# Two-layer hybrid decoder trunk on one core: stick-breaking sums in wider matmuls, a stacked short block of the latents, and another order of VectorE's and GpSimd's work between the output projection and the MLP

## The chip, the cores and the metric

One core of a Trainium2 chip runs one program. The metric is the device time of one execution in microseconds (us). The kernel before was timed in three runs: median 666.29, lowest 665.9, highest 666.32. PE is TensorE, DVE is VectorE, ACT is ScalarE, POOL is GpSimd, SP is the engine that issues most of the transfers.

## The reference, cut to what matters

Two layers (DEPTH = 2) over 256 tokens (two token tiles of 128) of width 1024. Each layer has four head groups of 4 heads x 64, one output projection, a gated MLP with a causal convolution, and a gated per-layer embedding. Three places of a layer matter here:

```python
# group A: stick-breaking attention
log_keep = jnp.where(mask, jax.nn.log_sigmoid(-z), 0.0)
shifted = jnp.concatenate([log_keep[..., 1:], jnp.zeros_like(log_keep[..., :1])], axis=-1)
tail = lax.cumsum(shifted, axis=3, reverse=True)
w = jnp.where(mask, jnp.exp(log_beta + tail), 0.0)
# group B: latents of rank 192 (queries) and 128 (keys, values), normalised, then projected up
c_q = rms_norm(mla[..., :192], mla_q_norm[i]);  c_kv = rms_norm(mla[..., 192:320], mla_kv_norm[i])
q_m = c_q @ mla_w_uq[i];                        kv_m = c_kv @ mla_w_ukv[i]
# between the attention and the MLP
x = x + groups.reshape(B, S, MIX_WIDTH) @ w_o[i]
h = rms_norm(x, ffn_norm[i])                    # then h @ w_up[i]
# at the end of a layer; p @ ple_proj can be computed at any time before
x = x + (p[i] @ ple_proj[i]) * jax.nn.sigmoid(x @ ple_gate[i])
```

## The kernel before, in words

**Weights.** All weights arrive in "units" of at most 128 x 2048 f32 through six slots of `raw`. A weight is used as two float32r numbers: ACT copies `raw` into a rounded high part (`high(u)`, L592), and DVE (`low(u)`, L1715) or POOL (`low(u)`, L460, for the units from `U_POOL` on) subtracts it from `raw` and leaves the low part in `wl`. A product of two such split operands is three matmuls into one sum (`split_product`, L966 to L968): high by high, high by low, low by high. Each engine has its own written order of instructions, with waits on counting semaphores (`F[...]`); nothing reorders them at run time.

**Stick-breaking sums (PE, L1298 to L1318).** With keys on the partitions, the sums along the keys are matmuls by a constant triangle `neg_tri_r` and, for the later key tile, a constant block `neg_ones_r`. Banks 4 and 5 of PSUM hold two heads each, 256 columns a head; bank 6 holds the four heads' later tile. For each bank and each of its two heads there are four matmuls: triangle by `sp_h` and by `pt_r` (256 columns each), ones by the high and the low part of the later tile (128 columns each). Bank 6 follows with two matmuls of 512 columns. ACT then takes the exponentials. PE goes on with `mla_T(1)` (L1286), the projection `M_SWA_B`, the first group's values (L1331), the scores, `o_turned`, transposes, the unit `M_MOBA_V`, and `group_T(0)` (L1342), which waits for `group_done`, made by DVE's `group_norm(0)` (L1811) after a root by POOL (L452). POOL comes to that root after `low(U_WO)` (L460) and two roots of other groups.

**Latents.** DVE scales the 192 and 128 columns (L1871, two instructions a token tile, `lat_done`); PE transposes them in three blocks of 128, 64 and 128 columns (L1226); ACT copies them as high parts `cT_h`, DVE subtracts for low parts `cT_l` (L1883). The second block has 64 rows of data and is multiplied with 128 rows of `uq`, of which POOL sets the lower 64 to zero. Each token tile takes 3 + 3 matmuls of 384 columns for the queries and 3 of 512 for keys and values.

**From the output projection to the MLP (the middle).** Four quarters of x (token tile, half of the columns) lie in PSUM banks 0 to 3. DVE adds each to x (`add_to_x`, L2003), ACT squares it with a sum (`x_square`, L573), and for each token tile POOL adds two sums (L467), makes the mean (L447) and takes the power -0.5 (L470; `x_root`). DVE's `norm(1)` writes hn = x * root * gain by quarters (L1652), PE transposes them (`x_T`, L1018), ACT and DVE make high and low parts, and the first unit of the MLP (`up(0, 0)`, L1504) starts. DVE's order is: addition 0, `low(U_FFN)` (a whole unit), additions 1 to 3, then the four hn. Between, PE has the product p @ ple_proj as filling: `project_p(0)`, `project_p(1)`, x_T of quarters 0 and 1, `project_p(2)`, x_T of quarters 2 and 3, `project_p(3)`; each `project_p` is six matmuls of 512 columns.

Of the kernel before, what the change touches and what calls it, by code (L numbers as in the profile page):

```python
# [15 lines left out]
P = 128  # L16
# [5 lines left out]
H = 4  # L22
# [16 lines left out]
MLA_COLS = QR + KVR + PE_DIM  # L39

# [64 lines left out]
def _cols(n):  # L105
# [25 lines left out]
    "x_squared": 8, "roots": 15, "hn_ready": 4, "xT_ready": 12, "hT_ready": 4, "roots_wide": 1, "row_root": 1,  # L131
    "xT_high": 12, "xT_low": 12, "pr_ready": 6, "squared": 7, "sums_ready": 4, "ssk_ready": 1,
    "lat_done": 2, "lat_T": 2, "cT_ready": 2, "mla_up": 2, "mla_up_ready": 4, "v_ready": 6,
    "mla_qk": 2, "mla_T": 2, "mT_ready": 4, "rrow_ready": 1, "uq_zero": 1, "up_high": 2, "up_low": 2, "cT_low": 2, "proj_high": 2, "proj_low": 2, "mla_high": 1, "mla_low": 1, "mla_a_high": 1, "mla_a_low": 1, "sbq_high": 1, "sbq_low": 1, "moba_qk": 1,
# [8 lines left out]
    "x_done": 4, "tables": 1, "sg_landed": 16, "uq_landed": 16, "uq2_landed": 16,  # L143
# [29 lines left out]
def build(nc, x_in, p_cols, positions, w_in, w_uq, w_ukv, attn_cols, norm_gains,  # L173
          small_gains, w_o, w_up, conv_cols, w_down, ple_proj, ple_gate, out):
    with ExitStack() as ctx:
# [241 lines left out]
        def _(pool):  # L417
# [36 lines left out]
            for layer in range(DEPTH):  # L454
# [50 lines left out]
                if layer == 0:  # L505
                    pool.memset(uq[QR - P:P, 1, :], 0.0).then_inc(consts_made, 1)
                    pool.wait_ge(consts_made, 13)
                    for z in (qk_sb, qk_moba, qk_swa):
                        pool.memset(z[:, 0:H, :], 0.0).then_inc(consts_made, 1)
                    pool.wait_ge(consts_made, 16)  # L510
# [57 lines left out]
        def _(act):  # L568
            act.dma_start(gcol[:], attn_cols).then_inc(gcol_landed, 16)
            def x_square(i):  # L570

                t, c = quarter(i)
                return act.activation(hn[:, t, c], x[:, t, c], ACT.Square,  # L573
                                      accum_out=stat(ST_X + i))

            for layer in range(DEPTH):
# [142 lines left out]
                act.wait_ge(F["uq2_landed"], base["uq2_landed"] + 16)  # L719
                act.wait_ge(F["ukv_landed"], base["ukv_landed"] + 16)  # L720
                if layer == 0:
                    act.wait_ge(consts_made, 13)
                else:
                    act.wait_ge(F["uq_zero"], layer)
# [221 lines left out]
        def _(pe):  # L946
            pe.sem_inc(w_used, RING)
            pe.wait_ge(consts_made, 12)
            for layer in range(DEPTH):
# [273 lines left out]
                for t in range(TT):  # L1223
                    pe.wait_ge(F["lat_done"], base["lat_done"] + t + 1)
                    for n, (c, w) in enumerate(((0, P), (P, QR - P), (QR, KVR))):
                        mm = pe.transpose(ps[0:w, 4 + t, n * P:(n + 1) * P], pr[:, 0, t, c:c + w],  # L1226
                                          ident[:])
                    mm.then_inc(F["lat_T"], 1)
                project_T(M_SB_K, 3, columns=(1,))
                if layer == 0:  # L1230
                    pe.wait_ge(consts_made, 16)
# [68 lines left out]
                for b in range(2):  # L1300
                    for j in range(2):
                        i = 2 * b + j
                        h = PAIRED[i]
                        o = ps[:, 4 + b, j * 256:(j + 1) * 256]
                        pe.matmul(o, neg_tri_r[:], sp_h[b][:, j * 256:(j + 1) * 256],
                                  start=False, stop=False, skip_group_check=True)
                        pe.matmul(o, neg_tri_r[:], pt_r[:, i * 256:(i + 1) * 256],
                                  start=False, stop=False, skip_group_check=True)
                        pe.matmul(o[:, P:256], neg_ones_r[:], sp_h[2][:, h * P:(h + 1) * P],
                                  start=False, stop=False, skip_group_check=True)  # L1310
                        mm = pe.matmul(o[:, P:256], neg_ones_r[:],
                                       pt_r[:, 1024 + h * P:1024 + (h + 1) * P], start=False,
                                       stop=True, skip_group_check=True)
                    mm.then_inc(F["sb_minus"], 1)
# [146 lines left out]
                def project_p(n):  # L1461
# [3 lines left out]
                    for k in range(2):  # L1465
# [4 lines left out]
                                           k == 0, k == 1)  # L1470
                    if n < 3:
# [107 lines left out]
        def _(dve):  # L1579
# [64 lines left out]
            for layer in range(DEPTH):  # L1644
                base = before(layer)
                def norm(n):
# [59 lines left out]
                def low(u, halves=False):  # L1706

                    slot, n, c = u % DEEP, COLS[u], 0
                    if halves:
# [6 lines left out]
                       ALU.subtract).then_inc(l_made, 1)  # L1716

# [150 lines left out]
                for t in range(TT):  # L1868
                    for j, (c, w, g) in enumerate(((0, QR, S_QN), (QR, KVR, S_KVN))):
                        v = pr[:, 0, t, c:c + w]  # L1870
                        last = stt(v, v, stat(ST_L + 4 + 2 * j + t), sg[:, g:g + w], ALU.mult,  # L1871
                                   ALU.mult)
# [7 lines left out]
                for t in range(TT):  # L1880
                    dve.wait_ge(F["cT_ready"], base["cT_ready"] + t + 1)
                    tok = slice(t * P, (t + 1) * P)
                    tt(cT_l[:, :, tok], ps[:, 4 + t, 0:384].rearrange("p (k n) -> p k n", k=3),  # L1883
                       cT_h[:, :, tok].bitcast(F32), ALU.subtract).then_inc(F["cT_low"], 1)
# [8 lines left out]
                if layer == 0:  # L1893
                    dve.wait_ge(consts_made, 16)
# [213 lines left out]
```

## Time and profile before

| what | value |
| --- | --- |
| time, median of 3 runs | 666.29 us |
| profiled execution: its own time | 666.2 us |
| profiled execution: span, first to last instruction | 664.5 us |
| time outside the span | 1.7 us |
| mean granted clock of PE | 0.998 |
| busy in the span: PE, DVE, ACT, POOL | 654.1, 436.1, 423.8, 414.0 us |

The time outside of the span is taken as it is. PE matmuls are pipelined, so what a matmul costs is read from the distance between the starts of two neighbours and not from its duration. The start of each row is in us from the start of the span; the second layer repeats the first some 326.5 us later.

### The profile page before, as it was taken

Reading aid. Unit: us, or ns where it says so; the run is one execution under the profiler, and the core shown is the slowest. Engines: PE = TensorE matmul, PEld = TensorE weight load, DVE = VectorE, ACT = ScalarE, POOL = GpSimd, SP = SyncE. Lnnn points to the kernel's source line nnn. Section 1 sums busy time; section 2 is a strip of 40 time slices with the busy share of each in tenths; the row PEclk is TensorE's granted clock in tenths of the full one; section 3 lists DMA queues with packets and bytes.
Section 4 is the critical chain, followed back from the end, with each engine's and each line's share of the span. In section 5 each row is a group of like instructions: output and inputs, shape, how many; then the busy total and the mean of one; then the engine's idle time right before and its main releaser. Section 6 shows DMA issues by size and latency. Waiting matters only on the chain.

```text
span 664.5 us, 9585 instructions
## 1 busy us (share of the span) xinstructions
PE 654.1 (98%) x3800; PEld 563.4 (85%) x3800; DVE 436.1 (66%) x621; ACT 423.8 (64%) x633; POOL 414.0 (62%) x222
## 2 busy tenths in 40 slices
PE   7999999999999999999999999999999999999997
PEld 5988887888888888888889889878888888888885
DVE  6976878749898985003488588875688989910033
ACT  6669886676767675334474889746776767643342
POOL 5543610388888887987841373015888888889871
PEclk9999999999999999999999999999999999999999
DMA  9962134575555555553387421165555555555411
GB/s 321 374 232 64 66 109 160 186 236 190 190 189 191 191 190 189 190 190 107 108 292 236 157 96 66 65 205 176 190 190 190 190 191 190 191 190 189 159 33 63
DMA packets 74445, 115.18 MB, mean 173 GB/s; under 512 B 2336, under 2 KB 58272, under 8 KB 74144
## 3 DMA queue, kind: packets, MB, share of 16 engines
q1 hardware_dynamic: 73248, 111.75, 50.6%
q10 hardware_dynamic: 1152, 2.81, 1.2%
q8 instruction: 30, 0.49, 0.3%
q14 instruction: 15, 0.12, 0.1%
HBM read 113.51 MB, written 1.05 MB: 172 GB/s over the span
## 4 chain that ended last, share of the span: by engine, by line
PE 94%; DVE 4%; ACT 1%; DMA 1%; issue 0%; POOL 0%; ACTq 0%
PE ps L1515 24%; PE ps L966 14%; PE ps L968 14%; PE ps L967 14%; PE ps L1517 12%; PE ps L1018 2%; PE ps L1112 1%; PE ps L1138 1%; PE ps L980 1%; PE ps L1377 1%; DVE wl L1715 1%; PE ps L1053 1%; PE ps L1150 1%; DVE hn L2068 1%; PE ps L1538 1%; PE ps L1540 1%
## 5 line engine op out<-in xcount | busy, mean ns | idle before, releaser
L460 POOL TENSOR_TENSOR wl<-raw,wh 128x2048 fp32r<-128x2048 f32 (+1 forms) x74 | 333.6, 4514 | 81.4 <-ACT wh L592 81.4
L1515 PE MATMUL ps<-hT_hl,wh 128*128 128x512 f32 x688 | 238.6, 392 | 0.0
L592 ACT ACTIVATE wh<-raw 128x2048 fp32r<-128x2048 f32 (+1 forms) x102 | 186.1, 1828 | 76.8 <-PE ps L968 69.7
L1517 PE MATMUL ps<-hT_hl,wl 128*128 128x256 f32 x688 | 193.6, 281 | 0.0
L1515 PEld LDWEIGHTS ps<-hT_hl,wh 128*128 128x128 f32 x688 | 129.2, 188 | 28.0
L1517 PEld LDWEIGHTS ps<-hT_hl,wl 128*128 128x128 f32 x688 | 129.6, 188 | 0.0
L447 POOL TENSOR_SCALAR st<-st 128x2 f32<-128x2 f32 (+3 forms) x26 | 11.1, 428 | 113.3 <-ACT lat L667 61.2
L966 PE MATMUL ps<-wh,hT_hl 128*128 128x512 f32 (+1 forms) x216 | 79.8, 369 | 0.0
L968 PE MATMUL ps<-wh,hT_hl 128*128 128x512 f32 (+1 forms) x216 | 77.4, 359 | 0.0
L967 PE MATMUL ps<-wl,hT_hl 128*128 128x512 f32 (+1 forms) x216 | 77.4, 358 | 0.0
L2003 DVE TENSOR_TENSOR x<-x,ps 128x512 f32<-128x512 f32 x16 | 10.6, 686 | 99.5 <-PE ps L968 97.5
L1715 DVE TENSOR_TENSOR wl<-raw,wh 128x2048 fp32r<-128x2048 f32 (+1 forms) x28 | 57.6, 2062 | 0.1
L968 PE MATMUL ps<-wh,g_late 128*128 128x512 f32 x144 | 56.1, 389 | 0.0
L967 PE MATMUL ps<-wl,g_late 128*128 128x512 f32 x144 | 56.1, 389 | 0.0
L966 PE MATMUL ps<-wh,g_late 128*128 128x512 f32 x144 | 56.0, 389 | 0.0
L2032 DVE SCALAR_TENSOR_TENSOR pb<-ps,conv,pb 128x255 f32<-128x255 f32 (+1 forms) x96 | 39.6, 473 | 17.3 <-ACT pb L888 17.3
L966 PEld LDWEIGHTS ps<-wh,hT_hl 128*128 128x128 f32 x216 | 40.8, 189 | 7.2 <-DVE wl L1715 1.1
L968 PEld LDWEIGHTS ps<-wh,hT_hl 128*128 128x128 f32 x216 | 40.8, 189 | 6.1
L967 PEld LDWEIGHTS ps<-wl,hT_hl 128*128 128x128 f32 x216 | 40.8, 189 | 5.3
L2045 DVE TENSOR_TENSOR g_late<-pb,g_late 128x512 fp32r<-128x512 f32 x10 | 38.4, 3841 | 3.8 <-ACT g_late L901 3.8
L2045 DVE TENSOR_TENSOR g_late<-pt,g_late 128x512 fp32r<-128x512 f32 x8 | 37.0, 4629 | 2.4 <-ACT g_late L901 2.4
L879 ACT ACTIVATE qk_moba<-ps 128x512 f32<-128x512 f32 x22 | 13.2, 599 | 38.3 <-PE ps L1517 38.3
(311 smaller groups left out, 1177.0 us busy)
## 6 DMA issues: line engine op xcount, KB each, us to landing
raw<-w_up SPq DMA_DIRECT2D x44, 1024.0 KB, 5.1
raw<-w_down SPq DMA_DIRECT2D x22, 1024.0 KB, 4.8
raw<-w_in SPq DMA_DIRECT2D x16, 1024.0 KB, 8.9
raw<-w_o SPq DMA_DIRECT2D x6, 1024.0 KB, 5.0
raw<-ple_gate SPq DMA_DIRECT2D x6, 1024.0 KB, 4.9
raw<-w_in SPq DMA_DIRECT2D x4, 704.0 KB, 5.3
ng<-norm_gains ACTq DMA_DIRECT2D x2, 1024.0 KB, 6.7
raw<-w_o SPq DMA_DIRECT2D x4, 512.0 KB, 4.1
```

Of the source, the lines that this page charges most:

```text
L460: pool.tensor_tensor(wl[:, slot, 0:n], raw[:, slot, 0:n], w_high(u)[:, 0:n].bitcast(F32), ALU.subtract).then_inc(done, 1)
L592: act.activation(w_high(u)[:, c:n], raw[:, slot, c:n], ACT.Copy).then_inc(h_made, 1)
L879: act.activation(low_halves[half], ps[:, bank:bank + 2, SEQ:2 * SEQ], ACT.Copy).then_inc(F["low_copied"], 1)
L966: pe.matmul(dst, a_h, b_h, start=start, stop=False, skip_group_check=True)
L967: pe.matmul(dst, a_h, b_l, start=False, stop=False, skip_group_check=True)
L968: return pe.matmul(dst, a_l, b_h, start=False, stop=stop, skip_group_check=True)
L1018: mm = pe.transpose(ps[:, banks[k], j * P:(j + 1) * P], src[:, t, c:c + P], ident[:])
L1515: pe.matmul(both, high[:, c], hU_all[:, k].rearrange("p a n -> p (a n)"), start=k == 0, stop=False, skip_group_check=True)
L1517: mm = pe.matmul(o, wl[:, slot, c], hU_h[:, k, :], start=False, stop=k == KT - 1, skip_group_check=True)
L1715: tt(wl[:, slot, c:n], raw[:, slot, c:n], w_high(u)[:, c:n].bitcast(F32), ALU.subtract).then_inc(l_made, 1)
L2032: stt(o, ps[:, bank + j, 0:SEQ - d], conv[:, tap, f:f + 1], o, ALU.mult, ALU.add).then_inc(F[name], 1)
L2045: tt(g_low(s), cv[s % 2][:, 0:2, :], g_high(s).bitcast(F32), ALU.subtract).then_inc(F["g_low"], 1)
```

## The change

1. **Stick-breaking sums.** For banks 4 and 5, the two heads of a bank go in one matmul: four a bank instead of eight; columns 512, 512, 256, 256, the latter two with two pieces of 128 columns each in the moving operand and in PSUM.
2. **Latents.** The 64 columns of the short block are written twice beside each other (`LAT_TWICE`), so that its transpose has 128 rows; DVE turns the lower 64 rows of `cT_h` into the low part in place. `uq` is loaded into both halves by two transfers. The block's product is two matmuls instead of three. POOL's zero fill of `uq`, with ACT's waits for it, goes away. DVE has three instructions a token tile where L1871 had two, and two where L1883 had one.
3. **The middle, DVE and POOL.** DVE adds quarters 0, 1, 2, makes the first half of the first MLP unit's low part (`low_part(U_FFN, 0)`), adds quarter 3, and then does `norm`: the sum of two squares and the constant for tile 0 (`x_mean(0)`), hn of quarters 0 and 1, `x_mean(1)`, the second half of the low part, hn of quarters 2 and 3. POOL has only the power there. ACT squares with a scale of D ** -0.5, so that the sum is a mean.
4. **The middle, PE.** The first three matmuls of `project_p(2)` come ahead of x_T of quarters 0 and 1.

```diff
 def load_small(eng, layer):
-            eng.dma_start(uq[0:QR - P, 1, :], w_uq[layer][P:QR, :]
-                          ).then_inc(F["uq2_landed"], 16)
+            for rows in (slice(0, QR - P), slice(QR - P, P)):
+                eng.dma_start(uq[rows, 1, :], w_uq[layer][P:QR, :]).then_inc(F["uq2_landed"], 16)
...
 # POOL
                 def x_root(n, t):
-                    pool.wait_ge(F["x_squared"], base["x_squared"] + 4 * n + 2 * t + 2)
-                    chained(pool.tensor_tensor(stat(ST_X + 4 + t), stat(ST_X + 2 * t),
-                                               stat(ST_X + 2 * t + 1), ALU.add))
-                    chained(mean(ST_X + 4 + t, 1, D))
+                    if n:
+                        pool.wait_ge(F["mean_ready"], base["mean_ready"] + t + 1)
+                    else:
+                        pool.wait_ge(F["x_squared"], base["x_squared"] + 2 * t + 2)
+                        chained(pool.tensor_tensor(stat(ST_X + 4 + t), stat(ST_X + 2 * t),
+                                                   stat(ST_X + 2 * t + 1), ALU.add))
+                        chained(mean(ST_X + 4 + t, 1, 1))
                     pool.tensor_tensor(stat(ST_X + 6 + t), stat(ST_X + 4 + t), neg_half[:, 0:1],
                                        ALU.pow).then_inc(F["roots"], 1)
...
-                if layer:
-                    pool.wait_ge(F["tables"], layer + 1)
-                    pool.memset(uq[QR - P:P, 1, :], 0.0).then_inc(F["uq_zero"], 1)
-                    pool.wait_ge(F["uq_zero"], layer)
...
 # PE, latents
-                    for n, (c, w) in enumerate(((0, P), (P, QR - P), (QR, KVR))):
-                        mm = pe.transpose(ps[0:w, 4 + t, n * P:(n + 1) * P], pr[:, 0, t, c:c + w],
+                    for n, c in enumerate((0, LAT_TWICE, QR)):
+                        mm = pe.transpose(ps[:, 4 + t, n * P:(n + 1) * P], pr[:, 0, t, c:c + P],
                                           ident[:])
...
-                    for k in range(2):
-                        split_product(o, cT_h[:, k, tok], cT_l[:, k, tok], uq_h[:, k, :],
-                                      uq_l[:, k, :], k == 0, k == 1)
+                    split_product(o, cT_h[:, 0, tok], cT_l[:, 0, tok], uq_h[:, 0, :],
+                                  uq_l[:, 0, :], True, False)
+                    pe.matmul(o, cT_h[:, 1, tok], uq_h[:, 1, :], start=False, stop=False,
+                              skip_group_check=True)
+                    pe.matmul(o, cT_h[0:QR - P, 1, tok], uq_l[0:QR - P, 1, :], start=False,
+                              stop=True, skip_group_check=True)
...
 # PE, stick-breaking sums
                 for b in range(2):
-                    for j in range(2):
-                        i = 2 * b + j
-                        h = PAIRED[i]
-                        o = ps[:, 4 + b, j * 256:(j + 1) * 256]
-                        pe.matmul(o, neg_tri_r[:], sp_h[b][:, j * 256:(j + 1) * 256],
-                                  start=False, stop=False, skip_group_check=True)
-                        pe.matmul(o, neg_tri_r[:], pt_r[:, i * 256:(i + 1) * 256],
-                                  start=False, stop=False, skip_group_check=True)
-                        pe.matmul(o[:, P:256], neg_ones_r[:], sp_h[2][:, h * P:(h + 1) * P],
-                                  start=False, stop=False, skip_group_check=True)
-                        mm = pe.matmul(o[:, P:256], neg_ones_r[:],
-                                       pt_r[:, 1024 + h * P:1024 + (h + 1) * P], start=False,
-                                       stop=True, skip_group_check=True)
-                    mm.then_inc(F["sb_minus"], 1)
+                    o = ps[:, 4 + b, :]
+                    later = o.rearrange("p (j n) -> p j n", j=2)[:, :, P:SEQ]
+                    high, low = (sp.rearrange("p (h n) -> p h n", h=H)[:, b:b + 3:2, :]
+                                 for sp in (sp_h[2], pt_r[:, 1024:1536]))
+                    pe.matmul(o, neg_tri_r[:], sp_h[b], start=False, stop=False,
+                              skip_group_check=True)
+                    pe.matmul(o, neg_tri_r[:], pt_r[:, b * 512:(b + 1) * 512], start=False,
+                              stop=False, skip_group_check=True)
+                    pe.matmul(later, neg_ones_r[:], high, start=False, stop=False,
+                              skip_group_check=True)
+                    pe.matmul(later, neg_ones_r[:], low, start=False, stop=True,
+                              skip_group_check=True).then_inc(F["sb_minus"], 1)
...
 # PE, the middle
                 project_p(1)
+                project_p(2, (0,))
                 x_T(hn, AT_MIDDLE, ("hn_ready", 0), quarters=(0, 1))
-                project_p(2)
+                project_p(2, (1,))
...
 # DVE, the middle
+                    def x_mean(t):
+                        dve.wait_ge(F["x_squared"], base["x_squared"] + 4 * n + 2 * t + 2)
+                        stt(stat(ST_X + 4 + t), stat(ST_X + 2 * t), EPS, stat(ST_X + 2 * t + 1),
+                            ALU.add, ALU.add).then_inc(F["mean_ready"], 1)
+                    x_mean(0)
                     for i in range(4):
                         t, c = quarter(i)
+                        if i == 2:
+                            x_mean(1)
+                            between()
...
-                add_to_x("wo_done", U_PROJ - 1, "x_mid", (0,))
-                low(U_FFN)
-                add_to_x("wo_done", U_PROJ - 1, "x_mid", (1, 2, 3))
-                norm(1)
+                add_to_x("wo_done", U_PROJ - 1, "x_mid", (0, 1, 2))
+                low_part(U_FFN, 0)
+                add_to_x("wo_done", U_PROJ - 1, "x_mid", (3,))
+                norm(1, lambda: low_part(U_FFN, 1))
```

## Rows read from the trace of the kernel before

**Rows 1.** The page: the chain that ended last, by engine.

```profile
PE 94%; DVE 4%; ACT 1%; DMA 1%; issue 0%; POOL 0%; ACTq 0%
```

**Rows 2.** Who waited for whom, PE: us in total, times, longest.

```profile
PE ps L1018 <- DVE hn L1652: 0.8, 2, 0.4
```

**Rows 3.** Timeline and windows, stick-breaking sums: start, duration; the window's length and busy times.

```profile
59.33 0.33 PE L1305 MATMUL ps<-gT_h,neg_tri_r 128*128 128x256 f32 x1
59.50 0.28 PE L1307 MATMUL ps<-pt_r,neg_tri_r 128*128 128x256 f32 x1
59.62 0.22 PE L1309 MATMUL ps<-gT_l,neg_ones_r 128*128 128x128 f32 x1
59.68 0.28 PE L1311 MATMUL ps<-pt_r,neg_ones_r 128*128 128x128 f32 x1
...
58.84:61.23 2.39, 2.39 (x20) 2.24 (x19) 2.36 (x2) 2.39 (x4) 1.32 (x1) 1.00 0.52 122
```

**Rows 4.** Timeline, latents of layer 0: DVE's scaling and low parts, PE's products.

```profile
24.05 1.73 DVE L1871 SCALAR_TENSOR_TENSOR pr<-pr,st,sg 128x192 f32<-128x192 f32 x4 [0.80 <-POOL st L452]
...
27.85 1.01 DVE L1883 TENSOR_TENSOR pt_r<-ps,pb_r 128x384 fp32r<-128x384 f32 x2
...
30.02 0.34 PE L966 MATMUL ps<-uq_h,pb_r 128*128 128x384 f32 x1
30.20 0.34 PE L967 MATMUL ps<-uq_l,pb_r 128*128 128x384 f32 x1
```

**Rows 5.** Timeline, the middle of layer 0, all engines.

```profile
116.72 0.69 DVE L2003 TENSOR_TENSOR x<-x,ps 128x512 f32<-128x512 f32 x1 [1.01 <-PE ps L1377]
...
117.33 2.28 DVE L1715 TENSOR_TENSOR wl<-raw,wh 128x2048 fp32r<-128x2048 f32 x1
...
118.11 0.39 PE L968 MATMUL ps<-wh,hT_hl 128*128 128x512 f32 x1
...
119.53 1.88 DVE L2003 TENSOR_TENSOR x<-x,ps 128x512 f32<-128x512 f32 x3
119.69 0.39 PE L966 MATMUL ps<-proj_h,pT_h 128*128 128x512 f32 x1
...
121.05 0.19 POOL L467 TENSOR_TENSOR st<-st 128x1 f32<-128x1 f32 x1 [9.65 <-ACT hn L573]
...
121.60 0.56 POOL L470 TENSOR_TENSOR st<-st,neg_half 128x1 f32<-128x1 f32 x1
...
122.19 1.41 DVE L1652 SCALAR_TENSOR_TENSOR hn<-x,st,ng 128x512 f32<-128x512 f32 x2 [0.79 <-POOL st L470]
122.27 0.72 POOL L467 TENSOR_TENSOR st<-st 128x1 f32<-128x1 f32 x1
...
124.07 0.47 PE L966 MATMUL ps<-proj_h,pT_h 128*128 128x512 f32 x1
...
124.33 1.41 DVE L1652 SCALAR_TENSOR_TENSOR hn<-x,st,ng 128x512 f32<-128x512 f32 x2 [0.73 <-POOL st L470]
...
126.33 0.47 PE L966 MATMUL ps<-proj_h,pT_h 128*128 128x512 f32 x1
...
127.80 0.28 PE L1504 MATMUL ps<-hT_hl,wh 128*128 128x256 f32 x1
```

**Rows 6.** Timeline: POOL's short operations beside VectorE's long ones, both layers.

```profile
59.86 2.29 DVE L1715 TENSOR_TENSOR wl<-raw,wh 128x2048 fp32r<-128x2048 f32 x1
59.91 2.31 POOL L447 TENSOR_SCALAR st<-st 128x16 f32<-128x16 f32 x1 [14.73 <-DVE st L1732]
...
337.03 0.88 POOL L470 TENSOR_TENSOR st<-st,neg_half 128x1 f32<-128x1 f32 x1
```

**Rows 7.** Timeline before group_T(0), layer 0: POOL, DVE and PE.

```profile
68.16 5.14 POOL L460 TENSOR_TENSOR wl<-raw,wh 128x2048 fp32r<-128x2048 f32 x1 [0.45 <-ACT wh L592]
...
75.87 0.88 DVE L1811 SCALAR_TENSOR_TENSOR hn<-ps,st,ng 128x256 f32<-128x256 f32 x2 [0.95 <-POOL st L452]
...
77.08 0.60 PE L1342 MATMUL ps<-ident,hn 128*128 128x128 f32 x4
```

More of the change, by code:

```diff
@@ L39 @@
 MLA_COLS = QR + KVR + PE_DIM
+LAT_TWICE = 384
 SB, MLA, SWA, MOBA = range(4)
@@ L572, in x_square @@
                 t, c = quarter(i)
-                return act.activation(hn[:, t, c], x[:, t, c], ACT.Square,
+                return act.activation(hn[:, t, c], x[:, t, c], ACT.Square, scale=D ** -0.5,
                                       accum_out=stat(ST_X + i))
@@ L718, in _ @@
                 act.wait_ge(F["uq_landed"], base["uq_landed"] + 16)
-                act.wait_ge(F["uq2_landed"], base["uq2_landed"] + 16)
+                act.wait_ge(F["uq2_landed"], base["uq2_landed"] + 32)
                 act.wait_ge(F["ukv_landed"], base["ukv_landed"] + 16)
[L721 to L724, printed above, removed]
                 for o, w in ((uq_h, uq), (ukv_h, ukv)):
@@ L1230, in _ @@
                 if layer == 0:
-                    pe.wait_ge(consts_made, 16)
+                    pe.wait_ge(consts_made, 15)
                 pe.wait_ge(F["up_low"], base["up_low"] + 2)
@@ L1459, in _, with project_p @@
                 project_out(3, (3,))
-                def project_p(n):
+                def project_p(n, blocks=range(2)):
                     slot, _ = unit(U_PROJ)
                     t, half = divmod(n, 2)
-                    for k in range(2):
+                    for k in blocks:
                         c = slice(k * D + half * 512, k * D + half * 512 + 512)
@@ L1470, in project_p @@
                                            k == 0, k == 1)
+                    if k == 0:
+                        return
                     if n < 3:
@@ L1645, in _, with norm @@
                 base = before(layer)
-                def norm(n):
+                def norm(n, between):
+                    def x_mean(t):
[3 more added lines that the diff above has]
+                    x_mean(0)
                     for i in range(4):
                         t, c = quarter(i)
+                        if i == 2:
+                            x_mean(1)
+                            between()
                         dve.wait_ge(F["roots"], base["roots"] + 13 * n + t + 1)
@@ L1716, in low, with low_part @@
                        ALU.subtract).then_inc(l_made, 1)
+                def low_part(u, part):
+                    slot, n = u % DEEP, COLS[u] // 2
+                    c = slice(part * n, (part + 1) * n)
+                    dve.wait_ge(h_made, highs(layer, u))
+                    last = tt(wl[:, slot, c], raw[:, slot, c], w_high(u)[:, c].bitcast(F32),
+                              ALU.subtract)
+                    if part:
+                        last.then_inc(l_made, 1)
                 def group_low(n):
@@ L1868, in _ @@
                 for t in range(TT):
-                    for j, (c, w, g) in enumerate(((0, QR, S_QN), (QR, KVR, S_KVN))):
+                    for j, (c, w, g) in enumerate(((0, P, S_QN), (QR, KVR, S_KVN))):
                         v = pr[:, 0, t, c:c + w]
-                        last = stt(v, v, stat(ST_L + 4 + 2 * j + t), sg[:, g:g + w], ALU.mult,
-                                   ALU.mult)
+                        stt(v, v, stat(ST_L + 4 + 2 * j + t), sg[:, g:g + w], ALU.mult, ALU.mult)
+                    o = pr[:, 0, t, LAT_TWICE:LAT_TWICE + P].rearrange("p (a n) -> p a n", a=2)
+                    v, g = (a.unsqueeze(1).broadcast_to([P, 2, QR - P]) for a in (
+                        pr[:, 0, t, P:QR], sg[:, S_QN + P:S_QN + QR]))
+                    last = stt(o, v, stat(ST_L + 4 + t), g, ALU.mult, ALU.mult)
                     last.then_inc(F["lat_done"], 1)
@@ L1882, in _ @@
                     tok = slice(t * P, (t + 1) * P)
-                    tt(cT_l[:, :, tok], ps[:, 4 + t, 0:384].rearrange("p (k n) -> p k n", k=3),
-                       cT_h[:, :, tok].bitcast(F32), ALU.subtract).then_inc(F["cT_low"], 1)
+                    src = ps[:, 4 + t, 0:384].rearrange("p (k n) -> p k n", k=3)
+                    tt(cT_l[:, 0:3:2, tok], src[:, 0:3:2], cT_h[:, 0:3:2, tok].bitcast(F32),
+                       ALU.subtract)
+                    o = cT_h[QR - P:P, 1, tok]
+                    tt(o, src[QR - P:P, 1], o.bitcast(F32), ALU.subtract).then_inc(F["cT_low"], 1)
                 def sb_rooted(rows, heads, bank, scale):
@@ L1893, in _ @@
                 if layer == 0:
-                    dve.wait_ge(consts_made, 16)
+                    dve.wait_ge(consts_made, 15)
                 dve.wait_ge(F["rrow_ready"], base["rrow_ready"] + 1)
```

10 lines of the change are left out of this document (4 added, 6 removed).

## Prediction

> **What bounds the kernel now.** I read the page first: the profiled execution took 666.2 us, 664.5 in the span and 1.7 outside, and its median neighbour 666.29, so a sum made against 666.2 stands for the median within 0.1. The chain that ended last is 94% PE [rows 1]: PE runs a queue of matmuls nearly without a hole, so an edit counts only by what it takes from PE's stream, or by the holes that it opens or fills. The list of waits, filtered to PE, comes second: inside a layer the largest is that of the transposes of hn in the middle, 0.8 us over both layers by the profile [rows 2]. Third come timelines of the three stages that the change touches [rows 3 to 5], and last a timeline of POOL and DVE side by side [rows 6], because the change lets DVE run a long instruction while POOL has a short one to do.
>
> What is not shown as a wait is slack: whoever shortens PE's stream uses slack up. So for each saving I looked for the next wait of PE behind it, and for what that one's producer hangs on.
>
> **Stick-breaking sums: shorter by 0.50 a layer.** The columns stay as they are (3072 in banks 4 and 5); only the number of matmuls falls from 16 to 8. By the starts, a matmul of 256 columns is followed after 0.12 (59.50 to 59.62), the first of 128 after 0.06, and from the second of 128 to the next head it takes longer than 0.06: the whole stage, of which 1.88 falls on banks 4 and 5 and 0.51 on the two wide matmuls of bank 6, takes 2.39 [rows 3]. A 512-column matmul in a row of its like costs (119.69 - 118.11)/7 = 0.226 [rows 5]. Pure streaming after the change is 6 x 0.226 + 4 x 0.12 = 1.84, with some 0.05 at the entry (the 0.17 from 59.33 to 59.50 against 0.12) 1.89. Saved: 0.50. The moving operand and PSUM now come in two pieces of 128 columns, which no row here shows for float32r; a gain below 0.50 is therefore open down to nothing.
>
> The Trainium skill (TensorE: Matmul & The Clock Gate, "LDWEIGHTS (loading the stationary operand)") gives a weight load as its columns divided by 1.2 in ns, 107 ns for 128 columns whatever the rows, and says under "Back-to-back issue gap" that the spacing is set by both, load and stream. By it a 128-column matmul is bound by the next load, which agrees with the lengthening behind the second matmul of 128 but not with the 0.06 behind the first; by it alone the saving would be 8 x (0.107 - 0.053) = 0.43 instead of 0.50.
>
> **How much of that survives: 0.25 a layer.** The next wait of PE that does not hang on PE's own earlier work is group_T(0). It starts at 77.08; DVE's second instruction of group_norm(0) ends at 75.87 + 0.88 = 76.75, and a waiting engine starts about 0.08 after such an end, so at 76.83 at the earliest [rows 7]. What DVE does there hangs on a root by POOL, which comes behind POOL's low(U_WO) (68.16 to 73.30), which waited for ACT's high part, which ACT reached through its own queue of copies, exponentials and a whole-unit copy without a pause from before the sums. None of that moves when PE comes out of the sums earlier. Slack: 77.08 - 76.83 = 0.25. So 0.25 of the 0.50 becomes a new stall of PE at L1342. The second layer repeats this.
>
> **Latents: shorter by 0.34 a layer.** A token tile loses one matmul of 384 columns; two starts stand 0.17 to 0.18 apart [rows 4]; two tiles give 0.34. The remaining short matmul has 64 rows instead of 128, but as many columns: same price. The transposes are as many as before. DVE gets more to do ahead of PE: scaling takes 1.73 for four instructions in layer 0, with six of 128 columns some 0.3 more, and the low parts, 1.01 for two, become four, some 0.2 more [rows 4]. PE's first product started at 30.02 and the low parts were ready at 27.85 + 1.01 = 28.86, a cover of 1.16 minus 0.5: hidden; if the cover were gone it would cost up to 0.5 once. PE's savings here move the later ACT and DVE work along, since the stick-breaking scores on PE start that chain; so the 0.34 is kept whole. The second transfer of uq is small; ahead of it in SP's queue is nothing that waits for it, and behind it are the loads of units 4 and later in layer 0 and, in the MLP, loads that wait for slots anyway. ACT's copy of unit 4 has a pause of over 2 us behind it. The zero fill on POOL (0.4 us) was on nobody's path. All of these: nothing, above or below, up to 0.2.
>
> **The middle: longer by 0.30 a layer.** I lay the new order on the old clock of layer 0 [rows 5]. On DVE one addition follows another after 0.61 (116.72 to 117.33). Addition 0 at 116.72, 1 at 117.33; addition 2 needs bank 2, whose last matmul starts at 118.11 and takes 0.39, so 118.54. Half a low part is half of the 2.2 from 117.33 to 119.53, with its fixed part 1.13: 119.15 to 120.28. Addition 3: 120.28 to 120.89. x_mean(0) 0.16 and a step to POOL 0.08, power 0.56, a step back 0.03: hn 0 at 121.72, against 122.19 before. That is the gain that the shorter chain brings. hn 0 and 1 take 1.41, so hn 1 is ready at 123.13; x_mean(1) starts at 123.05 (the next instruction starts 0.08 ahead of the last one's end), and the second half of the low part right behind it, at 123.13, for 1.13 to 1.22.
>
> Here lies what decides. POOL's power for tile 1 would start at 123.05 + 0.16 + 0.08 = 123.29, when DVE's long subtraction is already running. The rows show what happens to POOL then: a tensor_scalar of 128x16 that starts 0.05 behind a 2.29 us subtraction takes 2.31 and ends with it; the add of 128x1 takes 0.72 beside hn against 0.19 alone; the power takes 0.88 at 337.03 beside DVE's work against 0.56 [rows 5, 6]. So the power waits for the end of the half, 124.26, and then needs 0.45 (between 0.3 and the full 0.56) and 0.04 to DVE: hn 2 at 124.75, against 124.33 before.
>
> The Trainium skill (SBUF — State Buffer, "Who interferes with whom") says that a DVE instruction with two SBUF inputs and a GpSimd instruction that reads SBUF exclude each other for a whole instruction, in the order in which they start. The trace agrees (2.31 beside 2.29). It is a rule against this order of work: without it hn 2 would start at 124.26.
>
> PE on the same clock: 12 matmuls of project_p(0) and (1) from 119.69 to 122.42; the moved three to 123.10, which fill the hole that stood ahead of hn 0. Quarter 0 at 123.10, quarter 1 at 123.52 (0.41 a quarter: hn 1 was ready at 123.60 and project_p(2) began at 124.07), the rest of project_p(2) from 123.93 to 124.72 (the first behind transposes takes 0.32). hn 2 ends at 124.75 + 0.75 = 125.50, quarter 2 at 125.56: a hole of 0.84. hn 3 ends at 126.16, quarter 3 from 126.22 to 126.63. project_p(3) takes 127.80 - 126.33 = 1.47, so up(0, 0) starts at 128.10 against 127.80: +0.30. The hole is moved from quarter 0 to quarter 2 and gets longer, since what ends last is hn 3. The high and low parts of the quarters and ACT's pp_out have their cover: the last quarter isn't needed ahead of up's ninth matmul, and DVE's low(U_FFN + 1) is wanted a whole half unit later.
>
> **Sum.** A layer: -0.34 - 0.50 + 0.25 + 0.30 = -0.29. Two layers: -0.58. 666.2 - 0.58 = 665.6 us, a difference of 0.09%. A measurement of this kernel tells about 0.2%, 1.33 us, from no change: I forecast no change that can be told.
>
> **The rivals.**
>
> *The power is not held up* (or DVE reaches x_mean(1) so that POOL gets in first). For it: a power that had begun ahead of DVE's instruction kept its own time. Against it: rows 6, and DVE's own order. Then hn 2 at 124.26, hn 3 ready at 125.67, quarter 3 from 125.73 to 126.14, up at 127.61: -0.19 instead of +0.30 a layer. Sum -0.78 a layer, 664.6.
>
> *The slack at group_T(0) is not what caps the sums' gain*, because POOL or ACT come earlier too. For it: ACT's squares of group 0 do follow PE. Against it: POOL came from low(U_WO), 2.5 us of work behind it. Then -0.54 a layer, 665.1.
>
> *The slower side: two pieces of 128 columns in float32r run at a rate of their own.* Four such matmuls a layer. With d more each, the layer is at -0.29 + 4d, less where the stall at group_T(0) swallows the first 0.25; it becomes slower by 1.33 in all from a net 0.67 a layer, that is at d = 0.24 and more, where they take three times the 0.12 of the plain one. At 0.40 more each: -0.34 + 0.30 - 0.50 + 1.60 = +1.06 a layer, 668.3. For it: no row shows this form. Against it: the turned outputs of o_turned are strided too, and transposes there are as far apart as elsewhere.
>
> *The gains fail.* The sums save nothing and the DVE steps come 0.2 later than I laid them: -0.34 + 0.50 = +0.16 a layer, 666.5.
>
> **How the numbers follow.** My forecast 0.50 (665.1 to 666.1 with the steps' bounds), the uncapped sums 0.15 (665.1), the power not held up 0.14 (664.6), with part of the first also below 664.96 if both of these meet; the gains fail 0.14 (666.5); the slower side 0.07 (668.3). For 8 in 10 the range reaches from 664.4 to 666.9: it takes in the first four cases and leaves out the slower side and what lies past the second. Faster by over 0.2% (below 664.96): the power not held up, and half of the uncapped cases in which a step besides is shorter, 0.24. Slower (above 667.6): 0.07. Within: 0.69.
>
> **What the profile after would show.** Sums: 1.9 us instead of 2.39 from the first L1305 to the first transpose of mla_T(1); if it is over 2.2, the pieces cost. A wait of PE for DVE's L1811 line ahead of group_T(0), some 0.25 in each layer, where there was none; if it is missing, the cap was wrong. Latents: 3.17 instead of 3.51 from the first product of 384 columns to M_SB_V. Middle: the wait of L1018 for hn moves from tile 0 to tile 1, with 1.1 in a layer; the power of tile 1 takes 1.2 to 1.6 us instead of 0.56, and ends 0.4 to 0.6 behind the second half of the low part. If it takes 0.56, the first rival is right. The prediction would be wrong above all if hn 2 started before 124.33 on this clock, counted from project_p(0)'s first matmul at 119.69 (4.64 us behind it).

## The result and the profile after

| | before | after |
|---|---|---|
| median of 11 executions, us | 665.90 (665.43 to 666.36) | 667.67 (667.48 to 669.71) |
| ratio, 95% interval | | 1.0029 [1.0020, 1.0039] |
| profiled execution, span / own time | 664.5 / 666.2 | 668.0 / 669.71 |

The kernel became slower by 1.77 us. The forecast was 665.6 with a range to 666.9, so it missed by 2.1, on the side to which it gave 0.07. As a change it was -0.58, laid on a before of 666.2 that is 665.90 here, so the change is missed by 1.77 + 0.58 = 2.35. One execution each of e3_middle and e11_middle2 below took over 930 us at a granted clock of 0.66 and is left out of their medians. The profiled execution of after is 2.0 above its own median: its first matmul of M_SB_Q starts at 19.63 instead of 17.66, while the first loads land. The readings below therefore measure stretches between two landmarks of one timeline, and leave that start out.

| stretch (layer 0 / layer 1), us | before | after | forecast |
|---|---|---|---|
| latents: first product of 384 columns to M_SB_V | 3.51 / 3.50 | 3.92 / 3.92 | 3.17 |
| sums: first triangle matmul to mla_T(1) | 2.39 / 2.39 | 1.95 / 1.95 | 1.89 |
| mla_T(1) to M_SWA_B's first matmul | 0.98 / 0.98 | 1.42 / 1.42 | 0.98 |
| first triangle matmul to group_T(0) | 18.24 / 18.23 | 18.23 / 18.23 | 17.99 |
| middle: project_p(0) to up(0, 0) | 8.11 / 8.10 | 8.42 / 8.42 | 8.41 |

The third stretch lies inside the fourth. From group_T(0) to project_p(0) it is 42.6 in both kernels. A layer is thus longer by 0.41 + 0 + 0.31 = 0.72, two layers by 1.44, where the forecast had -0.34 - 0.25 + 0.30 = -0.29 a layer.

The page of after, the chain that ended last; DVE and ACT have taken a larger part of it than in [rows 1]:

```profile
PE 88%; DVE 5%; ACT 3%; DMA 1%; issue 1%; POOL 1%; SPq 0%; ACTq 0%
```

Who waited for whom in after, PE (us in total, times, longest). The first line answers to [rows 2]; the third is new:

```profile
PE ps L1012 <- DVE hn L1660: 1.5, 2, 0.8
PE ps L974 <- DMA raw<-w_in: 0.9, 1, 0.9
PE ps L960 <- DVE wl L1723: 0.8, 2, 0.4
```

Windows of after: the sums, the stretch behind them, and the latents of layer 0 (length, busy us of PE, PEld, DVE, ACT, POOL, clock, DMA share, GB/s). The granted clock is 1.00 in all:

```profile
61.26:63.21 1.95, 1.95 (x11) 1.62 (x11) 1.92 (x2) 1.95 (x4) 0.88 (x1) 1.00 0.48 86
63.21:64.63 1.42, 1.04 (x10) 0.78 (x8) 1.42 (x2) 1.42 (x1) 1.42 (x1) 1.00 0.63 245
32.01:35.93 3.92, 3.92 (x18) 2.79 (x17) 3.83 (x5) 0.98 (x2) 0.00 (x0) 1.00 1.03 402
```

**Latents.** Timeline of after, layer 1, PE and its weight loads (PEld), answering to [rows 4]. Up to 359.81 each load starts with the matmul ahead of it, and matmuls are 0.17 to 0.18 apart. The load for 64 rows starts only with its own matmul, which comes 0.26 behind the one ahead; so does the load of the next 128-row matmul, 0.37 later. The load of 64 rows is itself no longer than the others (0.18 beside 0.19); what moved is its start:

```profile
359.63 0.34 PE L962 MATMUL ps<-uq_h,pt_r 128*128 128x384 f32 x1
359.63 0.19 PEld L1234 LDWEIGHTS ps<-uq_h,pb_r 128*128 128x128 f32 x1
359.81 0.34 PE L1234 MATMUL ps<-uq_h,pb_r 128*128 128x384 f32 x1
360.07 0.18 PEld L1236 LDWEIGHTS ps<-uq_l,pb_r 64*128 64x128 f32 x1 [0.25 <-issue]
360.07 0.44 PE L1236 MATMUL ps<-uq_l,pb_r 64*128 64x384 f32 x1
360.44 0.19 PEld L960 LDWEIGHTS ps<-ukv_h,pb_r 128*128 128x128 f32 x1 [0.19 <-issue]
```

**Sums.** Timeline of after, layer 0, PE and DVE, answering to [rows 3]. The next matmul follows 512 columns after 0.23 and 256 after 0.12, as elsewhere. Then mla_T is done early, and the unit M_SWA_B (unit 8) waits for its low part:

```profile
61.57 0.40 PE L1304 MATMUL ps<-pt_r,neg_tri_r 128*128 128x512 f32 x1
61.80 0.28 PE L1306 MATMUL ps<-gT_l,neg_ones_r 128*128 128x256 f32 x1
61.92 0.28 PE L1308 MATMUL ps<-pt_r,neg_ones_r 128*128 128x256 f32 x1
62.04 0.39 PE L1302 MATMUL ps<-gT_h,neg_tri_r 128*128 128x512 f32 x1
...
62.28 2.29 DVE L1723 TENSOR_TENSOR wl<-raw,wh 128x2048 fp32r<-128x2048 f32 x1
...
64.63 0.50 PE L960 MATMUL ps<-wh,hT_hl 128*128 128x512 f32 x1 [0.38 <-DVE wl L1723]
```

**Middle.** Timeline of after, layer 0, answering to [rows 5]. The second power starts 0.17 behind DVE's half and takes 1.47 instead of 0.56; hn 2 comes with it:

```profile
122.12 0.39 PE L960 MATMUL ps<-proj_h,pT_h 128*128 128x512 f32 x1
...
123.53 0.56 POOL L474 TENSOR_TENSOR st<-st,neg_half 128x1 f32<-128x1 f32 x1 [9.71 <-DVE st L1649]
124.12 1.42 DVE L1660 SCALAR_TENSOR_TENSOR hn<-x,st,ng 128x512 f32<-128x512 f32 x2 [0.67 <-POOL st L474]
125.45 0.15 DVE L1649 SCALAR_TENSOR_TENSOR st<-st 128x1 f32<-128x1 f32 x1
125.52 1.22 DVE L1731 TENSOR_TENSOR wl<-raw,wh 128x1024 fp32r<-128x1024 f32 x1
...
125.69 1.47 POOL L474 TENSOR_TENSOR st<-st,neg_half 128x1 f32<-128x1 f32 x1 [1.60 <-DVE st L1649]
127.20 1.41 DVE L1660 SCALAR_TENSOR_TENSOR hn<-x,st,ng 128x512 f32<-128x512 f32 x2 [0.45 <-POOL st L474]
128.00 1.32 PE L1012 MATMUL ps<-ident,hn 128*128 128x128 f32 x8 [0.75 <-DVE hn L1660]
130.54 0.28 PE L1502 MATMUL ps<-hT_hl,wh 128*128 128x256 f32 x1
```

### The profile page after: what moved, and what is told of

It is laid out like the page before. It is cut to its first block, busy times and chain, and to the rows that moved or that the text cites. A ratio compares the mean times of both kernels' runs of the same rounds, so it can differ in the third digit from the quotient of the medians.

```text
span 668.0 us, 9548 instructions
## 1 busy us (share of the span) xinstructions
PE 655.5 (98%) x3780; PEld 561.6 (84%) x3780; DVE 438.5 (66%) x635; ACT 424.7 (64%) x633; POOL 410.2 (61%) x212
## 4 chain that ended last, share of the span: by engine, by line
PE 88%; DVE 5%; ACT 3%; DMA 1%; issue 1%; POOL 1%; SPq 0%; ACTq 0%
PE ps L1513 24%; PE ps L960 13%; PE ps L962 13%; PE ps L961 13%; PE ps L1515 12%; PE ps L1106 1%; PE ps L974 1%; DMA raw<-w_in 1%; PE ps L1132 1%; PE ps L1012 1%; PE ps L1372 1%; DVE wl L1723 1%; DVE hn L1660 1%; POOL st L474 1%; PE ps L1047 1%
## 5 line engine op out<-in xcount | busy, mean ns | idle before, releaser
L448 POOL TENSOR_SCALAR st<-st 128x2 f32<-128x2 f32 (+3 forms) x22 | 9.4, 428 | 114.5 <-ACT lat L665 61.2
L1723 DVE TENSOR_TENSOR wl<-raw,wh 128x2048 fp32r<-128x2048 f32 (+1 forms) x26 | 52.9, 2039 | 0.2
```

The costliest lines, as they stand in the source:

```text
L1723: tt(wl[:, slot, c:n], raw[:, slot, c:n], w_high(u)[:, c:n].bitcast(F32), ALU.subtract).then_inc(l_made, 1)
```

## Experiments

Edits are against the changed kernel unless said otherwise. Each profile's stretches are the mean of both layers, in the order of the table above; "hole" is how much later than in before PE's first product of 384 columns starts, counted from M_SB_Q's first matmul (12.36 in before). Medians are of 11 executions, but of 10 for e2 and e11, 5 for e7 and one for e5, of which only the stretches are read.

| run | median; before beside it | ratio, 95% interval | latents | sums | to M_SWA_B | to group_T(0) | middle | hole |
|---|---|---|---|---|---|---|---|---|
| e1_rows128 | 666.48; 666.10 | 1.0007 [0.9999, 1.0016] | 3.21 | 1.94 | 1.43 | 18.26 | 8.43 | 0.57 |
| e2_latents | 667.05; 666.10 | 1.0020 [1.0011, 1.0029] | 3.92 | 2.39 | 0.98 | 18.23 | 8.10 | 0.02 |
| e3_middle | 666.79; 666.10 | 1.0009 [1.0000, 1.0018] | 3.51 | 2.38 | 0.98 | 18.23 | 8.43 | 0.09 |
| e4_sums | 666.27; 666.10 | 1.0014 [1.0004, 1.0023] | 3.51 | 1.95 | 1.42 | 18.22 | 8.11 | 0.02 |
| e6_half_last | 666.33; 665.82 | 1.0006 [0.9997, 1.0015] | 3.93 | 1.94 | 1.43 | 18.24 | 7.58 | 0 |
| e7_halves8 | 668.08; 665.82 | 1.0035 [1.0022, 1.0048] | 3.96 | 1.95 | 0.79 | 18.14 | 8.43 | 0.57 |
| e8_pair | 666.81; 665.82 | 1.0017 [1.0008, 1.0026] | 3.54 | 1.95 | 1.41 | 18.23 | 8.43 | 0.57 |
| e9_three | 664.84; 665.82 | 0.9984 [0.9975, 0.9993] | 3.19 | 1.94 | 0.79 | 18.15 | 7.59 | 0.41 |
| e5_half_waits | 668.52, one time; 665.87 | | 3.96 | 1.95 | 1.54 | 18.36 | 8.65 | 0.57 |
| e10_two | 664.78; 665.87 | 0.9985 [0.9976, 0.9994] | 3.20 | 1.95 | 1.42 | 18.24 | 7.57 | 0.95 |
| e11_middle2 | 665.01; 665.87 | 0.9988 [0.9979, 0.9997] | 3.51 | 2.39 | 0.98 | 18.26 | 7.57 | 0.07 |
| e12_latents2 | 665.53; 665.87 | 0.9996 [0.9988, 1.0005] | 3.20 | 2.39 | 0.98 | 18.24 | 8.11 | 0.58 |

### The short block with 128 rows (e1_rows128)

```diff
-pe.matmul(o, cT_h[0:QR - P, 1, tok], uq_l[0:QR - P, 1, :], ...)
+pe.matmul(o, cT_h[:, 1, tok], uq_l[:, 1, :], ...)
```

It adds the product of both low parts to the queries, which the kernels leave out; the count and the columns of the matmuls stay as they are.

> The changed kernel, with its last matmul of the short block over all 128 rows instead of 64 (the lower 64 rows of uq's low part are its copy, so the product gains low times low, a part of the true product that the reference's sum has too). Theory T (the 64-row matmul between 128-row ones costs PE some 0.37 a token tile, 0.75 a layer): the stage from the first product of 384 columns to unit M_SB_V falls from 3.92 to 3.17 us, and the time by 1.5 us, from 667.7 to 666.2. Rival S (the time went at the start, where the second transfer of uq stands ahead of the loads of layer 0): the stage may shorten, but the time stays above 667.

Timeline of this run, layer 1, the same place as above. The load runs ahead again and 0.17 to 0.18 lie between starts:

```profile
357.65 0.33 PE L1234 MATMUL ps<-uq_h,pb_r 128*128 128x384 f32 x1
357.66 0.19 PEld L1236 LDWEIGHTS ps<-uq_l,pb_r 128*128 128x128 f32 x1
357.83 0.33 PE L1236 MATMUL ps<-uq_l,pb_r 128*128 128x384 f32 x1
358.00 0.39 PE L960 MATMUL ps<-ukv_h,pb_r 128*128 128x512 f32 x1
```

The stretch is 3.16 in layer 1 and 3.25 in layer 0, 0.67 to 0.76 under after and near the forecast's 3.17. The only thing that differs is the number of rows. The time is 666.48 where theory T had 666.2. Rival S fails: the time is under 667, and M_SB_Q starts at 17.62 here and at 17.48 in e2 with both transfers of uq, and at 17.66 in before with one.

### Each part alone (e2_latents, e3_middle, e4_sums)

Edits: before with the hunks of one part only.

> The kernel before with the latents' part of the change alone (two transfers of uq, stacked short block, more instructions on VectorE, no zero fill). Theory T: 2 x 0.41 = +0.8 us, all of it between the first product of 384 columns and unit M_SB_V. Rival S: +2 us or more, with the start (until the first matmul of M_SB_Q) later by up to 2 us. What was predicted: -0.7.

> The kernel before with the middle's part alone (order of additions and halves on VectorE, means there, three matmuls of project_p(2) earlier). As predicted: +0.30 a layer, +0.6 us in all, with a power of 1.4 to 1.6 us for tile 1. Rival: the part gains in itself (-0.4) and the trace of the changed kernel only shows it beside something else.

> The kernel before with the stick-breaking sums by two heads alone. Theory C (the 0.44 saved is given back 1 us later, at the wait for the low part of M_SWA_B): no change, -0.1 to +0.1 us, with a wait of 0.35 to 0.45 at the first matmul of M_SWA_B in each layer. Rival: the wait in the changed kernel came from the other parts; then -0.5 to -0.9 us here.

Latents alone +0.95, middle alone +0.69, sums alone +0.17 by the medians, where +0.8, +0.6 and none were expected; they add up to 1.81 beside the 1.77 of the whole. The stretches change as they do in after, so the parts hardly touch each other. Five of e4's eleven times lie between 667.7 and 668.3 and the rest near 666, so its ratio is above its median's difference. The five are longer by about as much as after's profiled execution loses at its start, but no trace shows what made them. By the stretches the sums save 0.44 a layer and gain nothing: in e4, PE waits for the low part of unit 8. Timeline of e4, layer 0:

```profile
60.31 0.60 PE L1286 MATMUL ps<-ident,lat 128*96 128x128 f32 x4
60.75 0.60 PE L1286 MATMUL ps<-ident,hT 128*96 128x128 f32 x4
61.73 0.50 PE L966 MATMUL ps<-wh,hT_hl 128*128 128x512 f32 x1 [0.39 <-DVE wl L1713]
```

### The second half of the low part behind hn 3 (e6_half_last)

```diff
                         if i == 2:
                             x_mean(1)
-                            between()
...
                         stt(hn[:, t, c], ...)
+                    between()
```

> The changed kernel, with the second half of the low part behind hn 3 instead of ahead of hn 2. Theory L (the power of tile 1 waits for the end of VectorE's long subtraction): the power takes 0.56 instead of 1.47, hn 2 starts 0.8 behind x_mean(1) instead of 1.75, and the middle falls from 8.42 to about 7.55 (8.11 before the change): -1.7 us in all against the changed kernel, from 667.7 to 666.0. Rival: the power is slow for a reason of its own (it stays at 1.4 or so), and the middle falls by 0.2 at most.

Timeline of this run, layer 0: the second power takes 0.56 again, hn 2 starts 0.83 behind x_mean(1), and the half comes last.

```profile
123.17 0.15 DVE L1649 SCALAR_TENSOR_TENSOR st<-st 128x1 f32<-128x1 f32 x1
123.41 0.56 POOL L474 TENSOR_TENSOR st<-st,neg_half 128x1 f32<-128x1 f32 x1 [1.60 <-DVE st L1649]
124.00 1.42 DVE L1659 SCALAR_TENSOR_TENSOR hn<-x,st,ng 128x512 f32<-128x512 f32 x2 [0.67 <-POOL st L474]
125.34 1.22 DVE L1731 TENSOR_TENSOR wl<-raw,wh 128x1024 fp32r<-128x1024 f32 x1
```

The middle is 7.57 to 7.58, which is 0.85 less than in after and 0.53 less than in before. The time is 666.33 where theory L had 666.0; its rival, a power that stays at 1.4, is out.

### The half behind the root's wait (e5_half_waits)

```diff
                         if i == 2:
                             x_mean(1)
-                            between()
                         dve.wait_ge(F["roots"], ...)
+                        if i == 2:
+                            between()
```

> The changed kernel, with the second half of the low part behind the wait for tile 1's root and still ahead of hn 2. VectorE is idle while POOL has the power. Theory L: the power takes 0.56 instead of 1.47, and hn 2 starts x_mean(1) + 0.8 + 1.15 = 1.95 behind (1.75 in the changed kernel): the middle gets 0.2 longer (8.6). Rival (the power is slow because of something else in this place): it stays at 1.4 and the middle gets longer by 1 us or more.

Timeline of this run, layer 0: the power is free of the half, but the half now stands ahead of hn 2.

```profile
123.82 0.56 POOL L474 TENSOR_TENSOR st<-st,neg_half 128x1 f32<-128x1 f32 x1 [1.60 <-DVE st L1649]
124.41 1.22 DVE L1732 TENSOR_TENSOR wl<-raw,wh 128x1024 fp32r<-128x1024 f32 x1 [0.67 <-POOL st L474]
125.55 1.41 DVE L1661 SCALAR_TENSOR_TENSOR hn<-x,st,ng 128x512 f32<-128x512 f32 x2
```

The middle is 8.65, which is 0.23 more than in after. So it is the half itself, 1.14 between starts, that must leave the way to hn 2; letting the two run side by side costs the 0.91 by which the power gets longer, 0.23 less than putting the half in front.

### The low part of unit 8 in two halves (e7_halves8)

```diff
-low(8)
+for a in range(2):                      # columns 0:1024, then 1024:2048
+    tt(wl[:, 8 % DEEP, c], raw[:, 8 % DEEP, c], w_high(8)[:, c].bitcast(F32),
+       ALU.subtract).then_inc(l_made if a else F["half_low"], 1)
...
-project(M_SWA_B, SWA_BANKS, 0)
+project_tile(M_SWA_B, 0, SWA_BANKS, 0, part=range(0, 2), half=True)
+project_tile(M_SWA_B, 0, SWA_BANKS, 0, part=range(2, 4))
+project_tile(M_SWA_B, 1, SWA_BANKS, 0)
```

> The changed kernel, with the low part of unit M_SWA_B in two halves on VectorE, and TensorE's first two blocks waiting for the first half alone. Theory C (the sums' 0.44 a layer is given back at this wait): the wait of 0.4 goes, PE gets to group_T(0) 0.2 to 0.25 earlier, and waits 0.15 to 0.2 there for hn, as the prediction had it: -0.5 us in all. Rival: no second cap, -0.8 us in all, no wait at group_T(0).

The wait at M_SWA_B is gone, and another one is there, 15 us later. Who waited for whom in this run, PE:

```profile
PE ps L1342 <- DVE hn L1834: 0.8, 2, 0.5
```

M_SWA_B now starts 0.79 behind mla_T(1), 0.63 earlier than in after and 0.19 less than the 0.98 of before: PE stood there for 0.19 in before too. From the sums to group_T(0) it is 18.03 and 18.24, so that of 0.44 + 0.19 freed ahead of it 0.2 is left in one layer and nothing in the other. The -0.5 us that theory C had is missed: the time is no better than that of after (668.08, of five executions, beside 667.67).

### Both 64-row matmuls side by side (e8_pair)

```diff
 for t in range(TT):
     ...                                  # three products of the long block
     pe.matmul(o, cT_h[:, 1, tok], uq_h[:, 1, :], ...)
-    pe.matmul(o, cT_h[0:QR - P, 1, tok], uq_l[0:QR - P, 1, :], ...)
+for t in range(TT):
+    pe.matmul(ps[:, 4 + 2 * t, 0:H * QK], cT_h[0:QR - P, 1, tok], uq_l[0:QR - P, 1, :], ...)
+for t in range(TT):
     ...                                  # the products with ukv
```

> The changed kernel, with the two 64-row matmuls of the two token tiles side by side (the products of keys and values behind them). Theory W (the cost is in going from 128 to 64 rows and back): the stage falls from 3.92 to about 3.55, -0.7 us in all. Rival R (each 64-row matmul is slow by itself): the stage stays at 3.9.

Timeline of this run, layer 1:

```profile
357.60 0.34 PE L1234 MATMUL ps<-uq_h,pb_r 128*128 128x384 f32 x1
357.86 0.29 PEld L1238 LDWEIGHTS ps<-uq_l,pb_r 64*128 64x128 f32 x2 [0.25 <-issue]
357.87 0.62 PE L1238 MATMUL ps<-uq_l,pb_r 64*128 64x384 f32 x2
358.41 0.50 PE L960 MATMUL ps<-ukv_h,pb_r 128*128 128x512 f32 x1
358.75 0.39 PE L961 MATMUL ps<-ukv_l,pb_r 128*128 128x512 f32 x1
```

The two 64-row matmuls end 0.62 - 0.44 = 0.18 later than one (0.44 in after), the usual distance, and both their loads are done 0.29 after the first began, so the second one runs ahead of its matmul again. The entry costs 0.27 instead of 0.17, and the exit is as long as in after (0.34 between the two with ukv instead of 0.23), and both are paid once instead of twice: 3.50 to 3.58 instead of 3.92. The price belongs to the change of size, not to a matmul of 64 rows. The time falls with it, to 666.81 (-0.86 against after, -0.7 expected).

### Versions put together (e9_three, e10_two, e11_middle2, e12_latents2)

e9 is e1, e6 and e7 in one; e10 is e1 and e6; e11 is before with the middle of e6 alone; e12 is before with the latents of e1 alone.

> The changed kernel with all three mends: 128 rows in the short block, the second half of the low part behind hn 3, unit M_SWA_B's low part in halves. By the sum of the single ones: against the changed kernel -1.2 (measured) - 1.7 - 0.5 = -3.4 us, 664.3; against the kernel before -1.6 to -2.4. If the parts stand in each other's way, less.

> The changed kernel with 128 rows in the short block and the second half of the low part behind hn 3, but unit M_SWA_B's low part whole. If the halves of that unit bring nothing (e7), the time is that of e9, 664.8; if their gain was hidden in e7, 0.4 us more.

> The kernel before with the middle's part alone, and the second half of the low part behind hn 3. By e6's trace the middle falls from 8.11 to 7.57: -1.1 us, 664.7 to 664.8. Rival: something later takes it back, and the time stays within 0.3 of before.

> The kernel before with the latents' part alone, its last matmul over 128 rows. As predicted for the latents: -0.34 a layer, -0.7 us, less up to 0.5 once in layer 0, where VectorE's longer chain ends about when PE wants the low parts (a hole of 0.3 in e1). Rival: the stage keeps a cost of the stacking itself, and the time stays at 666 or above.

e10 is the best of the simple ones: 1.09 us under before, an interval wholly below 1. e9, with the halves of unit 8 besides, is no faster (664.84, where the sum of the single effects had 664.3). Alone, the middle gives -0.86, with an interval below 1 as well. The latents alone give -0.34, half of the -0.7 expected, and their interval takes in 1.

## Why the prediction was wrong

**Latents: the step that failed.** "The remaining short matmul has 64 rows instead of 128, but as many columns: same price." That was the term of -0.34 a layer, and it measured +0.41: 0.75 a layer, 1.5 us of the 2.35 by which the change was missed. A change of the row count costs on the way in and on the way out, and there the weight load no longer starts ahead of its matmul (0.26 and 0.37 between starts instead of 0.17 and 0.17, and 0.34 instead of 0.23 behind that), shown by e1, which removes the cost by row count alone, and by e8, which pays it once instead of twice by pairing. I counted this edit among the sure ones: it had a row for the columns, none for the rows, and no bound upward. The Trainium skill (TensorE: Matmul & The Clock Gate, "The mechanism" in Part 3) says that a weight load is pulled ahead of running matmuls when it targets a row group that doesn't conflict, or the background weight buffer. The trace fits the second of these: loads of 128 rows start 0.17 to 0.18 ahead of their matmul, beside one that uses the same rows. The load that changes the row count doesn't run ahead.

**The latents' cover in layer 0: mis-sized, and a second condition missed.** I put 0.5 on DVE's longer way against a cover of 1.16. Six scalings instead of four, and four low parts instead of two, make it 5.58 in e1 instead of 4.81 (24.05 to 28.86, [rows 4]), so 0.77. Timeline of e1, layer 0, DVE, then PE's last product before and the first one behind the wait, 0.40 apart instead of 0.12:

```profile
24.71 0.78 DVE L1889 SCALAR_TENSOR_TENSOR pr<-pr,st,sg 128x128 f32<-128x128 f32 x2 [0.81 <-POOL st L453]
...
30.00 0.29 DVE L1908 TENSOR_TENSOR pb_r<-ps,pb_r 64x128 fp32r<-64x128 f32 x1
...
30.15 0.28 PE L962 MATMUL ps<-hT_hl,wl 128*128 128x256 f32 x1
30.55 0.41 PE L960 MATMUL ps<-uq_h,pb_r 128*128 128x384 f32 x1
```

The 0.77 alone would still be hidden. What it meets is a start that moves from one execution to another: counted from M_SB_Q's first matmul, DVE begins to scale 6.39 later in before and 6.34 and 6.40 later in e2 and e6, which have no hole, but 6.93 to 7.47 later in the seven experiments with a hole of 0.41 to 0.95, where PE's product follows 5.83 to 5.85 behind that start each time. e3 and e11 begin as late as 7.09 and 7.10 but without the latents' part, and have 0.09 and 0.07. So it takes both, the longer way and a late start; what moves the start was not followed. After's own profiled execution begins to scale at 5.27 and has no hole, and its median holds a rest, 1.77 - 1.44 = 0.33. That this rest is the hole was not shown by a trace of a median execution; it stays an argument, and the interval of the difference (1.3 to 2.6) takes in 1.44 as well.

**Sums: the saving right (0.44 for 0.50), the cap in the wrong place and too mild.** "The next wait of PE that does not hang on PE's own earlier work is group_T(0)": there was a nearer one, at M_SWA_B, 1 us behind the sums, for the low part of unit 8 that starts at 59.86 in [rows 6] and ends at 62.15. PE starts there at 62.21 in before, 0.06 behind that end, as it does in after, where it waits (64.57 to 64.63). There was no slack at all: PE waited there already, 0.20 by its weight load's row below and 0.19 by e7, though the list of PE's waits leaves it out. So all of the 0.44 is given back, and the wait of 0.25 forecast at group_T(0) isn't in after. I had the row of DVE and read only its effect on POOL. Timeline of before, PE's rows that go with it:

```profile
62.21 0.19 PEld L966 LDWEIGHTS ps<-wh,hT_hl 128*128 128x128 f32 x1 [0.20 <-DVE wl L1715]
62.21 0.50 PE L966 MATMUL ps<-wh,hT_hl 128*128 128x512 f32 x1
```

The cap at group_T(0) exists as well, as e7 showed once the first was out of the way. Strided pieces of 128 columns cost nothing here. So the slower side, given 0.07, came true by time (667.67) but not by the mechanism that I had named for it.

**Middle: right.** +0.31 for +0.30; the power took 1.47 (1.2 to 1.6 was said), and hn 2 started 5.08 behind project_p(0)'s first matmul (5.06 was laid). PE's wait for it was 0.75 a layer: the working had 0.84, the list of signs 1.1, which doesn't follow from it. The rival in which the power isn't held up would have given a middle of 7.92 with this order; after has 8.42, so it is out. That the power's length hangs on the half is shown by e6 and e5, where it is 0.56 again. The Trainium skill's rule (SBUF — State Buffer, "Who interferes with whom"), that the two exclude each other, agrees with this: 1.47 beside a half of 1.22.

By steps: 1.5 us from the latents' rows, 2 x 0.25 = 0.5 from the sums, 0.02 from the middle. That is 2.0 of the 2.35, and the other 0.33 is the rest named above, for which no trace stands. The chance of 0.24 for the faster side was not added up rightly either: its two terms give 0.14 + 0.075 = 0.215.

## What to carry to other kernels

A block's row count is a price of its own: before one short matmul is put among full ones, count the changes of size, fill the rows up if what lies there is harmless, or keep short ones together. Before a saving is booked, go through the next microseconds of that engine's queue instruction by instruction and put beside each the end of the slowest thing it needs; a place that the list of waits leaves out can be a wait already, as the 0.20 in the weight load's row was here. Where GpSimd has a short step on the path, give VectorE's long two-operand work a place behind the instruction that needs the step's result, as e6 and e10 did (0.85 a layer under after, 0.53 under before), not between them.

## What the runs showed of the hardware

- A matmul over 64 rows between ones over 128 (384 columns) cost 0.38 more: with two of them the stretch was 3.92 instead of 3.16 in layer 1 (after, e1), and with the two side by side 3.50 (e8). PEld shows it: the load starts with its matmul, idle for 0.25 ahead, instead of with the one before.
- Operand and PSUM in two pieces of 128 columns with a gap ran at the plain rate in after: the next matmul starts 0.11 to 0.13 behind these 256 columns, and 0.23 to 0.24 behind 512 in one piece.
- A power on POOL that starts 0.17 behind a 1.22 us subtraction on DVE with two SBUF operands ends 0.42 behind its end (127.16 against 126.74, after): of the 0.56 that it takes alone, 0.42 came after the subtraction.
